# VectorE's two-tensor operations written as tensor times 1.0, then tensor; three sums over partitions taken as rounded part plus remainder

## The reference, cut to what matters

```python
h = rmsnorm(x, pre_norm_g)
proj = einsum('btd,dn->btn', h, w_in)                 # 2048 x 7168
q, fz, iv, gate_a, u, ug, gate_b = split(proj)
# group A, per head: scores under decay, state, then
o = o * rsqrt(mean(o*o, axis=-1) + EPS) * norm_g      # mean over 128 features of a head
o_a = o * silu(gate_a)
# group B
a = u * sigmoid(ug);  y = causal_conv31(a) + dw_b     # 1024 channels
mu  = mean(y, axis=-1)
var = mean(square(y - mu), axis=-1)
y = (y - mu) * rsqrt(var + EPS) * ln_g + ln_b
o_b = silu(y) * silu(gate_b)
out = x + rmsnorm(concat(o_a, o_b) @ w_out, post_norm_g)
```

## Time and profile before

| what | value |
|---|---|
| median of 3 runs | 859.86 us |
| profiled execution, device time | 859.81 us |
| its span, first to last instruction | 858.1 us |
| TensorE busy | 845.8 us (99%) |
| VectorE busy | 644.8 us (75%) |
| ScalarE busy | 446.9 us (52%) |
| GpSimd busy | 402.7 us (47%) |
| granted TensorE clock, mean | 0.997 |

### The profile page before, as it was taken

The page is one execution under the profiler, slowest core; times in us unless marked ns, Lnnn a source line. Parts: engine busy times, 40 slices in busy tenths (PEclk is TensorE's granted clock), DMA queues, the critical chain, the costliest instruction groups (busy, mean ns, idle before and its releaser), DMA issues.

```text
span 858.1 us, 12144 instructions
## 1 busy us (share of the span) xinstructions
PE 845.8 (99%) x4162; PEld 709.7 (83%) x4162; DVE 644.8 (75%) x1033; ACT 446.9 (52%) x692; POOL 402.7 (47%) x209
## 2 busy tenths in 40 slices
PE   8999999999999999999999999999999999999996
PEld 7978888888888888888888888888888888888885
DVE  4668789998989994957758496684947893787557
ACT  7854444453432366646646564574656842554442
POOL 3588778799746345242533425244243444032000
PEclk9999999999999999999999999999999999999998
DMA  9999976879405224141331324223231256888945
GB/s 309 249 208 250 241 148 159 201 168 209 123 26 147 83 65 123 51 122 50 98 98 49 98 66 118 60 80 91 63 108 49 79 165 198 223 146 171 268 198 196
DMA packets 127135, 119.15 MB, mean 139 GB/s; under 512 B 3408, under 2 KB 102009, under 8 KB 124537
## 3 DMA queue, kind: packets, MB, share of 16 engines
q1 hardware_dynamic: 117289, 88.24, 33.7%
q0 software_dynamic: 9056, 25.17, 15.9%
q10 hardware_dynamic: 752, 5.25, 1.6%
HBM read 103.96 MB, written 4.19 MB: 126 GB/s over the span
## 4 chain that ended last, share of the span: by engine, by line
PE 96%; ACT 1%; DVE 1%; POOL 1%; issue 0%; DVEq 0%; POOLq 0%; ACTq 0%
PE banks L1704 19%; PE banks L1706 19%; PE banks L1705 19%; PE banks L1737 6%; PE banks L1738 6%; PE banks L1736 6%; PE banks L1849 3%; PE banks L1848 3%; PE banks L1847 3%; PE banks L1647 2%; PE banks L1768 1%; PE banks L1758 1%; PE banks L1616 1%; PE banks L1774 1%; PE banks L1802 1%; PE banks L1777 1%
## 5 line engine op out<-in xcount | busy, mean ns | idle before, releaser
L527 POOL TENSOR_TENSOR w_lo<-w_raw,w_hi 128x1024 fp32r<-128x1024 f32 x122 | 309.6, 2547 | 320.1 <-ACT w_hi L661 300.0
L1704 PE MATMUL banks<-h_hi,w_hi 128*128 128x512 f32 x736 | 291.2, 396 | 0.7 <-POOL w_lo L527 0.7
L1706 PE MATMUL banks<-h_hi,w_lo 128*128 128x512 f32 x736 | 286.7, 390 | 0.0
L1705 PE MATMUL banks<-h_lo,w_hi 128*128 128x512 f32 x736 | 286.5, 389 | 0.0
L1166 DVE SCALAR_TENSOR_TENSOR banks<-work,tap,banks 128x512 f32<-128x512 f32 x238 | 179.8, 755 | 7.9
L1704 PEld LDWEIGHTS banks<-h_hi,w_hi 128*128 128x128 f32 x736 | 138.3, 188 | 29.2 <-POOL w_lo L527 1.1
L1706 PEld LDWEIGHTS banks<-h_hi,w_lo 128*128 128x128 f32 x736 | 138.1, 188 | 29.1
L1705 PEld LDWEIGHTS banks<-h_lo,w_hi 128*128 128x128 f32 x736 | 138.3, 188 | 28.1 <-issue 0.5
L661 ACT ACTIVATE w_hi<-w_raw 128x1024 fp32r<-128x1024 f32 x105 | 110.5, 1052 | 92.8 <-PE banks L1706 51.9
L1847 PE MATMUL banks<-w_hi,h_hi 128*128 128x512 f32 x128 | 50.8, 397 | 0.0
L1849 PE MATMUL banks<-w_hi,h_lo 128*128 128x512 f32 x128 | 49.9, 390 | 0.0
(11 more groups left out here) (232 smaller groups left out, 1305.0 us busy)
## 6 DMA issues: line engine op xcount, KB each, us to landing
w_raw<-in_w_in SPq DMA_DIRECT2D x112, 512.0 KB, 3.8
w_raw<-in_w_out SPq DMA_DIRECT2D x32, 512.0 KB, 5.0
gates<-in_w_in POOLq DMA_DIRECT2D x12, 512.0 KB, 7.7
work<-in_w_out POOLq DMA_DIRECT2D x12, 512.0 KB, 10.2
work<-h_hi POOLq DMA_DIRECT2D x4, 1024.0 KB, 9.8
work<-h_lo POOLq DMA_DIRECT2D x4, 1024.0 KB, 10.3
mix<-in_x ACTq DMA_DIRECT2D x4, 1024.0 KB, 9.9
out_y<-mix SPq DMA_DIRECT2D x3, 1024.0 KB, 3.9
```

The lines of the kernel that those rows point to most:

```text
L527: g.tensor_tensor(w_lo[:, a], w_raw[:, r * UW:(r + 1) * UW], w_hi[:, a].bitcast(fp32), ALU.subtract).then_inc(lo_done, 1)
L1704: mm(o, wh, hh, start=kt == 0, stop=False)
L1705: mm(o, wh, hl, start=False, stop=False)
L1706: ins = mm(o, wl, hh, start=False, stop=kt == KT - 1)
```

## The change

On VectorE a helper `merge` takes the place of nearly every `tensor_tensor`: `(one * 1.0) op two` instead of `one op two`, with the same tiles and the same shapes. Some with a PSUM input (L1201, L1215, L1441, L1479, L1526) and the small ones at the start stay. The three fp32 sums over partitions become two fp32r matmuls each (`column_sums`), with a rounded part by ScalarE and a remainder by VectorE. The mean's moves from after unit 4 to after unit 5 of head 0, the variance's from after unit 0 to after unit 2 of head 1, and `ln_rstd` from step 1 to step 3. `late` at step 1 makes `t4` after the four score copies instead of ahead of them. In the output loop ScalarE's `out_hi(7)` moves behind `late` and `mix_hi(15)`.

```diff
+        ysum_parts, vacc_parts, last_sq_parts = zip(side_hi, side_lo)
@@ scalar, late
-                    if not last:
-                        act.wait_ge(osq_done, 2 * g + 1)
-                        A(sq_hi, t4, ACT.Copy).then_inc(osq_hi, 1)
+                    act.wait_ge(osq_done, 2 * g + 1)
+                    A(last_sq_parts[0] if last else sq_hi, t4, ACT.Copy).then_inc(osq_hi, 1)
@@ scalar, head 0
                 head_step(0, u, (N_HEAD - NO_RAW) // RING)
+                if u == 4:
+                    act.wait_ge(ysum_done, J)
+                    A(ysum_parts[0], lnr, ACT.Copy).then_inc(ysum_hi, 1)
@@ scalar, head_rest
-                    if first and u == 1:
+                    if first and u == 3:
                         ln_rstd()
                     late(h - 1, u, first)
+                    if first and u == 0:
+                        act.wait_ge(vacc_done, J)
+                        A(vacc_parts[0], t3, ACT.Copy).then_inc(vacc_hi, 1)
@@ scalar, output loop
-                if s:
+                if s not in (0, 7):
                     out_hi(s)
...
+                if s == 7:
+                    out_hi(s)
@@ vector
+            def merge(to, one, two, op):
+                return V.scalar_tensor_tensor(to, one, 1.0, two, ALU.mult, op)
...
-                    V.tensor_tensor(t3, t3, sq, ALU.add).then_inc(vacc_done, 1)
+                    merge(t3, t3, sq, ALU.add).then_inc(vacc_done, 1)
...
-                        V.tensor_tensor(cut(lev[n], m, 0), ref, even, ALU.subtract)
+                        merge(cut(lev[n], m, 0), ref, even, ALU.subtract)
...
-                V.tensor_tensor(w_lo[:, a], src, w_hi[:, a].bitcast(fp32), ALU.subtract).then_inc(fast_lo, 1)
+                merge(w_lo[:, a], src, w_hi[:, a].bitcast(fp32), ALU.subtract).then_inc(fast_lo, 1)
@@ vector, late: the two lines on t4 move from here to behind take_scores
-                if u == 1:
-                    dve.wait_ge(gate_s, 3 * (g + 1))
-                    V.scalar_tensor_tensor(t4, sgate, 0.0, t4, ALU.min, ALU.subtract).then_inc(gate_ls, 1)
...
-                if u == SQ_U and not last:
+                if u == SQ_U:
                     dve.wait_ge(osq_hi, g + 1)
-                    V.tensor_tensor(sq_lo, t4, sq_hi.bitcast(fp32), ALU.subtract).then_inc(osq_done, 1)
+                    hi, lo = last_sq_parts if last else (sq_hi, sq_lo)
+                    merge(lo, t4, hi.bitcast(fp32), ALU.subtract).then_inc(osq_done, 1)
@@ vector, head 0 behind own
+                if u == 3:
+                    dve.wait_ge(ysum_hi, 1)
+                    merge(ysum_parts[1], lnr, ysum_parts[0].bitcast(fp32), ALU.subtract).then_inc(ysum_lo, 1)
@@ vector, head_rest behind late
+                    if first and u == 1:
+                        dve.wait_ge(vacc_hi, 1)
+                        merge(vacc_parts[1], t3, vacc_parts[0].bitcast(fp32), ALU.subtract).then_inc(vacc_lo, 1)
@@ tensor
+            def column_sums(to, parts):
+                mm(to, ones_r[:, :], parts[0], start=True, stop=False)
+                return mm(to, ones_r[:, :], parts[1], start=False, stop=True)
...
-                    if last:
-                        pe.wait_ge(osq_done, 2 * g + 1)
-                        mm(XB, ones[:, :], t4, start=True, stop=True).then_inc(norm_done, 1)
-                        return
...
-                    if first and u == 4:
-                        pe.wait_ge(ysum_done, J)
-                        mm(bank(2), ones[:, :], lnr, start=True, stop=True).then_inc(mean_done, 1)
-                    if second and u == 0:
-                        pe.wait_ge(vacc_done, J)
-                        mm(bank(3), ones[:, :], t3, start=True, stop=True).then_inc(var_done, 1)
+                    if first and u == 5:
+                        pe.wait_ge(ysum_lo, 1)
+                        column_sums(bank(2), ysum_parts).then_inc(mean_done, 1)
+                    if second and u == 2:
+                        pe.wait_ge(vacc_lo, 1)
+                        column_sums(bank(3), vacc_parts).then_inc(var_done, 1)
```

More of the change, by code:

```diff
@@ L1174, in add_to_sum @@
                     dve.wait_ge(ysum_done, j)
-                    V.tensor_tensor(lnr, lnr, y, ALU.add).then_inc(ysum_done, 1)
+                    merge(lnr, lnr, y, ALU.add).then_inc(ysum_done, 1)
             def finish_conv(j, r, s):
@@ L1188, in v_third_sum @@
                 dve.wait_ge(v_added[u], V_LANDED["P6"])
-                V.tensor_tensor(v_raw("P7", u), v_bsum[u], v_raw("P7", u), ALU.subtract).then_inc(v_third, 1)
+                merge(v_raw("P7", u), v_bsum[u], v_raw("P7", u), ALU.subtract).then_inc(v_third, 1)
             def v_join(kind, out, pair, joins=0, minus=False, less=False):
@@ L1261, in ln_tile @@
                     V.tensor_copy(lnp[:, :], par3[:, TAPS + 1:TAPS + 3, j]).then_inc(ln_v, 1)
-                    V.tensor_tensor(t1, y, lnr, ALU.mult).then_inc(ln_x, 1)
+                    merge(t1, y, lnr, ALU.mult).then_inc(ln_x, 1)
                     dve.wait_ge(ln_v, 7 * j + 1)
@@ L1270, in ln_tile @@
                     dve.wait_ge(ln_v, 7 * j + 4)
-                    V.tensor_tensor(t3, t3, t4, ALU.add).then_inc(ln_v, 1)
-                    V.tensor_tensor(t2, t1, gb, ALU.mult).then_inc(ln_v, 1)
+                    merge(t3, t3, t4, ALU.add).then_inc(ln_v, 1)
+                    merge(t2, t1, gb, ALU.mult).then_inc(ln_v, 1)
                 if s == 2:
@@ L1275, in ln_tile @@
                     dve.wait_ge(ln_v, 7 * j + 6)
-                    V.tensor_tensor(y, t2, t3, ALU.mult).then_inc(ln_v, 1)
+                    merge(y, t2, t3, ALU.mult).then_inc(ln_v, 1)
             def own(h, u, first):
@@ L1295, in own @@
                     dve.wait_ge(f_v, 8 * h + 3)
-                    V.tensor_tensor(t2, t2, t1, ALU.add).then_inc(f_v, 1)
+                    merge(t2, t2, t1, ALU.add).then_inc(f_v, 1)
                     dve.wait_ge(f_v, 8 * h + 4)
@@ L1337, in level_diffs @@
                         ref = runs(bcum, RUN)[:, :, RUN - 1:RUN].broadcast_to([P, T // RUN, RUN])
-                        V.tensor_tensor(runs(lev[n], RUN), ref, runs(bcum, RUN), ALU.subtract).then_inc(lev_d, 1)
+                        merge(runs(lev[n], RUN), ref, runs(bcum, RUN), ALU.subtract).then_inc(lev_d, 1)
                     elif n == MID_Q:
@@ L1341, in level_diffs @@
                             ref = after(bcum, i - 1)[:, :, :, RUN - 1:RUN].broadcast_to([P, TT, GROUPS, MID_W[i]])
-                            ins = V.tensor_tensor(mid(lev[n], i), after(bcum, i), ref, ALU.subtract)
+                            ins = merge(mid(lev[n], i), after(bcum, i), ref, ALU.subtract)
                         ins.then_inc(lev_d, 1)
@@ L1356, in level_times @@
                         m = LEVELS[n]
-                        V.tensor_tensor(cut(lev[n], m, odd), cut(lev[n], m, odd), cut(what, m, odd), ALU.mult)
+                        merge(cut(lev[n], m, odd), cut(lev[n], m, odd), cut(what, m, odd), ALU.mult)
                     elif n == MID_K and not odd:
-                        V.tensor_tensor(lev[n], lev[n], what, ALU.mult)
+                        merge(lev[n], lev[n], what, ALU.mult)
                     elif n == MID_Q and odd:
                         for i in range(3):
-                            V.tensor_tensor(mid(lev[n], i), mid(lev[n], i), after(what, i), ALU.mult)
+                            merge(mid(lev[n], i), mid(lev[n], i), after(what, i), ALU.mult)
             def take_scores(g, k, src):
@@ L1473, in mix_lo @@
                 dve.wait_ge(mhi_done, at + 1)
-                V.tensor_tensor(tokens(h_lo, at), both_halves(mix[:, m * T:(m + 1) * T]), tokens(h_hi, at).bitcast(fp32),
+                merge(tokens(h_lo, at), both_halves(mix[:, m * T:(m + 1) * T]), tokens(h_hi, at).bitcast(fp32),
                                 ALU.subtract).then_inc(mlo_done, 1)
@@ L1497, in sum_sides @@
                     dve.wait_ge(m_summed, M_SUM[n - 1, at])
-                V.tensor_tensor(out, a, b, op).then_inc(m_summed, 1)
+                merge(out, a, b, op).then_inc(m_summed, 1)
             def raw_of(step):
@@ L1507, in side_rest @@
                 dve.wait_ge(side_his, i + 1)
-                V.tensor_tensor(side_lo[i % SIDES].rearrange("p (k t) -> p k t", k=2), side(kind, u),
+                merge(side_lo[i % SIDES].rearrange("p (k t) -> p k t", k=2), side(kind, u),
                                 side_hi[i % SIDES].bitcast(fp32).rearrange("p (k t) -> p k t", k=2), ALU.subtract).then_inc(side_los, 1)
@@ L1575, in _ @@
                     dve.wait_ge(joined, JOINED["u2"])
-                    V.tensor_tensor(pair_c12, pair_c12, pair_c21, ALU.add).then_inc(joined, 1)
+                    merge(pair_c12, pair_c12, pair_c21, ALU.add).then_inc(joined, 1)
                 if (kind, u) == ("P3", 1):
```

27 lines of the change are left out of this document (15 added, 12 removed).

## The result

The changed kernel takes 860.75 us (median of 20 runs, 860.39 to 861.92), the kernel before on the same chip 859.38 us (20 runs): a ratio of 1.0015, 95% interval [1.0009, 1.0021]. It is 1.4 us slower. That is inside the 0.2% that I called no change, but the interval keeps clear of 1, and 860.75 lies above my range, which ended at 860.5. The profiled execution took 860.57 us, its span 858.9, 0.8 more than before.

A forecast was written before the change was run, and what follows sets the result against it. TensorE, busy 845.8 of 858.1 us, was taken to bound the kernel; 859.81 less 1.24 for the three sums, all else at nothing, gave 858.57, shown as a median of 858.6 us, range 858.1 to 860.5.

The forecast's parts named there:

- Part 1: Three fp32 sums on TensorE, each replaced by two fp32r matmuls: 0.41 us saved each, 1.24 us in all.
- the forecast's 1.24 us: The whole gain predicted on TensorE, from the three sums together, with nothing taken off for waits.
- rival 2: The last norm's chain is late and a lock makes TensorE wait 0.4 us: 859.0 us, chance 6%.
- rivals 1 and 3: Slower merges delay GpSimd's remainder for unit 67, 860.5 us, 7%; all merges at half rate, about 885 us, 2%.
- unit 67: Weights unit whose GpSimd remainder waits behind VectorE's two-input operations: cover predicted to shrink from 2.47 to 1.37 us.
- Output unit 7: Last output unit, where TensorE needs `h_lo`: its 0.54 us of cover was expected to stay or grow.
- Part 3 (c): `out_hi(7)` behind the last norm: GpSimd's unit starts at about 724 instead of 719.9, still covered, at no cost.
- Part 3 (a): `ln_rstd` waits for the variance in head 1: ScalarE's step 3 comes 3.7 us later, hidden by 10 us of cover.
- Part 2: Copy and merge that the three new pairs wait for: ready before TensorE asks, so nothing was taken for them.
- Part 3 (b): `t4` behind the score copies: ScalarE gets it 6 us later, fitting ahead of its idle 7.16 us, at no cost.
- Rival 4: A move priced at nothing makes TensorE wait 0.5 us or more per head: 862 or above; 7% with any other wait.

The follow-up runs named there:

- e8: The changed kernel with the rounding of weights for step 4 of head 1 ahead of the root and t4 ahead of the score copies: 858.31 us, ratio 0.9985.
- e5: The kernel before with only the merges, 30 tensor_tensors of VectorE in the new form: 859.53 us, ratio 0.9998.
- e4: The changed kernel with only ScalarE's rounding of weights for step 4 of head 1 put ahead of the root: 858.68 us, ratio 0.9989.
- e2: The changed kernel with only the gate's step t4 put back ahead of the four score copies: 860.50 us, ratio 1.0010.

## Why the prediction was wrong

**What was right.** TensorE's own count sets the end. The three sums gave -0.46, -0.43 (-0.59 - 0.30 + 0.60 - 0.14) and -0.45, where I had 0.41 each, so Part 1 holds; e8's steps show that the forecast's 1.24 us was there to be had. None of the three new pairs waits: the mean's remainder ends at 303.72, and TensorE comes at 306.16; the variance's at 328.36 and TensorE at 337.78; the last norm's is ready at 717.0 at the latest and used at 719.72, 2.7 us of cover or more against the 3.2 that I had. So rival 2 did not come. The merges cost 13 ns per 1024 columns, beside 1223 in the earlier trace rows, and nothing when strided (417 ns in the first row here; 415 for L1357's products in the kernel before):

```profile
L1094 DVE SCALAR_TENSOR_TENSOR work<-work 128x256 f32<-128x256 f32 x128 | 48.2, 417 | 0.3
...
L1094 DVE SCALAR_TENSOR_TENSOR w_lo<-w_raw,w_hi 128x1024 fp32r<-128x1024 f32 x22 | 27.1, 1236 | 20.9 <-ACT w_hi L1011 20.9
```

With that, and with e5, rivals 1 and 3 fall. From 730 to 835 us VectorE has 71.12 us of work, 71.88 in the earlier trace rows. The rule of the Trainium skill ("Vector Engine (DVE) Microarchitecture Reference", section 7), by which this form would halve the throughput with two fp32 SBUF sources, is not borne out at 256, 512 or 1024 columns. That a merge still locks the port was right too: GpSimd's op ahead of unit 67 takes 5.59 us, 5.00 in the earlier trace rows,

```profile
305.03 5.59 POOL L529 TENSOR_TENSOR w_lo<-w_raw,w_hi 128x1024 fp32r<-128x1024 f32 x1 [7.48 <-ACT w_hi L663]
```

it ends at 310.62 and TensorE comes at 312.06: 1.44 us of cover, where I had 1.37. Output unit 7 has 0.93 us, where I said that its 0.54 would stay or grow. Part 3 (c) came as priced: GpSimd's unit there begins at 725.00 instead of 719.89, and TensorE does not wait.

**The step that failed: Part 3 (a),** "Its last product of a head ends at 417.34 and TensorE asks at 427.39: 10 us of cover", and "the rounding of weights queued behind is as much later, with 10 us or more to TensorE's use of those units". ScalarE's step 3 came 3.0 us later, where I had 3.7. Against the kernel before this costs VectorE nothing, the scans even began 0.79 us sooner; but VectorE's work follows TensorE, which is 1.8 us earlier there than before, and in the rows above it stands idle for ScalarE 0.69 and 0.78 us. Two things were not seen:

- I measured the cover to the last result of VectorE's chain. The chain holds another one that TensorE needs sooner, the remainder of head 0's square, and its cover was 0.81 us, a twelfth. I looked for thin places at unit 67, at the new pairs and at output unit 7, and not at the pair that was there already.
- I asked of the later rounding only when TensorE needs its unit. But behind it GpSimd runs for 2.4 us, and 3 us later means other neighbours: VectorE's scans, 3.54 us instead of 1.37. I had the lock in hand, from the earlier trace rows, and used it for the merges alone.

A third thing enlarged it: the time that TensorE gains ahead of such a place is taken out of its cover. Here 0.89 us of gain (-0.46, -0.89, +0.46) stood ahead of slot 6. That alone is more than the 0.81 us of cover; without a collision VectorE comes sooner too, and e4 has 0.25 us left. So what I had in Part 2, that nothing is paid for, has to be asked of all waits behind a gain, not of the new ones.

**Part 3 (b)** failed on a smaller scale by the same omission. I read the copies and the gate's step in one head of the loop, where it takes 0.71 us, and not in the last head, which runs beside the output units and where GpSimd works beside it: 2.60 us, and 0.47 us on TensorE.

Rival 4 had "a move that I priced at nothing", but once per head; it was two moves, once each. The largest gap in the prediction was thus that no case stood for a move that shifts GpSimd against VectorE.

Sum by measured terms: 859.81 - 1.34 + 2.09 + 0.47 = 861.0; with the first stage's 0.49 less, 860.5, beside 860.57 measured.

## What to carry to other kernels

Where a change makes the bounding engine faster and moves work on the others, list every result that this engine takes from another behind the first gain, with its cover, old ones and last iterations too, and take the gain off each. Where an instruction is moved, follow it through to the GpSimd or VectorE operation that it releases, and look what lies beside that one at its new time. Here a gain of 1.3 us was outspent by two waits of 2.6 us together, each behind one VectorE instruction that met one of GpSimd. Moving one rounding of weights ahead of the root took away the larger wait, and moving the gate's step back the other.

## What the runs showed of the hardware that was not expected

- The lock hits the scans too: four `TENSOR_TENSOR_SCAN` of 128 columns take 1.37 us alone and 3.44 to 3.54 us when a remainder of GpSimd begins beside them. One scan takes it all, 2.50 to 2.58 us instead of 0.4. The loss, 1.9 to 2.2 us, is most of GpSimd's 2.4 us, whether the scans, a merge (2.85 us for 0.69) or the gate's step (2.60 for 0.69) meet it. In the change GpSimd began 0.27 us behind the first scan and went through at full speed, 2.36 us.
- A wait of TensorE costs more than the idle time that the profile gives. Idle 1.81 us moved the starts by 2.09, idle 0.32 by 0.60, idle 0.20 by 0.47: each time 0.27 to 0.28 more. The rows show what it is. Idle time is counted from the end that the profile gives the matmul before, 363.53 at slot 6, but the next could have started at 363.37, 0.23 us behind its start; that is 0.16 us. And the first matmul behind the wait holds the engine 0.33 us (365.34 to 365.67) instead of 0.23; in the last head, with 192 columns, 0.27 instead of 0.16. The last 0.01 to 0.02 us are spread over the matmuls behind it.
- Executions of one program differ by some tenths of a microsecond in the first stage, ahead of all that was changed: -0.7 to +0.5 us against the one trace of the kernel before. The change and e2 are the same program up to 320 us, and 0.96 us apart there, more than some of the differences studied here. Steps in the starts of TensorE's units repeat to 0.1 us, and are the better measure below 1 us.
